# A two-direction RWKV mixer: state walk reordered, one direction's token-laid data in the other half, values reversed by four products

## What is computed

```python
def rwkv7_scan(r, w, k, v, kk, bb, s0, reverse):
    def step(s, inp):
        r_t, w_t, k_t, v_t, kk_t, b_t = inp
        sa = jnp.einsum('bhij,bhj->bhi', s, kk_t)
        s = s * w_t[:, :, None, :] - sa[..., None] * b_t[:, :, None, :] + v_t[..., None] * k_t[:, :, None, :]
        return s, jnp.einsum('bhij,bhj->bhi', s, r_t)
    ...

for d in range(2):
    tc = rwkv_dir_terms(pc[0], pc[1], pc[2], pc[3][d], pc[4][d], ...)
    tl = rwkv_dir_terms(pl[0], pl[1], pl[2], pl[3][d], pl[4][d], ...)
    s_ctx, yc = rwkv7_scan(*tc[:6], zeros, d == 1)
    _, yl = rwkv7_scan(*tl[:6], s_ctx, d == 1)
    oc = oc + yc + tc[6]
    ol = ol + yl + tl[6]
```

## Time and profile before

| | |
|---|---|
| time, median of 3 runs | 2403.95 us (2402.38 to 2406.59) |
| span of the profiled execution | 2404.0 us |
| TensorE busy, weight loads | 2280.8 us, 1700.4 us |
| VectorE, ScalarE, GpSimd busy | 1744.5, 636.9, 236.2 us |
| mean granted TensorE clock | 0.988 of 2.4 GHz |
| first record of the first walk, of the last walk | 1408.3 us, 1889.8 us (L3048) |

### The profile page before, as it was taken

One profiled execution on the slowest core, in us unless ns is written; L12 is line 12 of the kernel. 1 busy time (PEld: TensorE's weight loads), 2 busy tenths in 40 slices (PEclk: granted clock), 3 DMA queues, 4 the chain that ended last, 5 costly groups with the idle time before them and its releaser, 6 DMA issues.

```text
span 2404.0 us, 40144 instructions
## 1 busy us (share of the span) xinstructions
PE 2280.8 (95%) x17202; PEld 1700.4 (71%) x17202; DVE 1744.5 (73%) x2951; ACT 636.9 (26%) x1318; POOL 236.2 (10%) x261
## 2 busy tenths in 40 slices
PE   7999989999997999999999999899998998999998
PEld 3586558888884688888755665766756754768975
DVE  3786477887799888878946869797797425767553
ACT  1314341111002311111033344544444412111111
POOL 2000000201541002024500000000000000000000
PEclk9999999999998999999999999999999999999999
DMA  8232335544532233343313000010010031221102
GB/s 341 74 119 97 140 114 174 172 165 163 177 130 80 79 130 122 135 149 127 118 64 120 23 36 21 23 36 22 21 34 6 20 121 70 88 70 53 36 18 105
DMA packets 43905, 227.95 MB, mean 95 GB/s; under 512 B 4752, under 2 KB 6928, under 8 KB 27600
## 3 DMA queue, kind: packets, MB, share of 16 engines
q1 hardware_dynamic: 23136, 140.56, 16.2%
q0 software_dynamic: 20016, 82.72, 10.1%
q10 hardware_dynamic: 576, 2.11, 0.3%
HBM read 219.07 MB, written 6.29 MB: 94 GB/s over the span
## 4 chain that ended last, share of the span: by engine, by line
PE 83%; DVE 12%; ACT 2%; issue 2%; DMA 1%; POOL 0%; ACTq 0%; DVEq 0%; POOLq 0%
PE ps L692 21%; PE ps L2349 10%; PE ps L914 7%; PE ps L3412 6%; PE ps L2127 3%; PE ps L1048 3%; PE ps L464 2%; PE ps L1747 2%; PE ps L2359 2%; PE ps L2368 2%; PE ps L3666 2%; PE ps L3863 2%; PE ps L3520 2%; PE ps L1249 1%; PE ps L3073 1%
## 5 line engine op out<-in xcount | busy, mean ns | idle before, releaser
L2349 PE MATMUL ps<-H,ring 128*128 128x256 f32 (+1 forms) x832 | 271.4, 487 | 5.4 <-ACT LW L2568 2.6
L692 PE MATMUL ps<-right_sums,left_sums 128*128 128x256 f32 x1056 | 242.8, 379 | 2.7 <-DVE left_sums L672 2.7
L2349 PEld LDWEIGHTS ps<-H,ring 128*128 128x128 f32 x832 | 157.4, 190 | 112.9 <-issue 92.8
L692 PEld LDWEIGHTS ps<-right_sums,left_sums 128*128 128x128 f32 x1056 | 200.5, 190 | 30.6 <-DVE left_sums L672 3.5
L692 PE MATMUL ps<-H,ring 128*128 128x256 f32 x704 | 164.7, 385 | 11.3 <-ACT H L635 11.3
L914 PE MATMUL ps<-G,ring 128*128 128x256 f32 x704 | 159.8, 379 | 0.0
L692 PEld LDWEIGHTS ps<-H,ring 128*128 128x128 f32 x704 | 135.1, 193 | 34.0 <-issue 11.5
L914 PEld LDWEIGHTS ps<-G,ring 128*128 128x128 f32 x704 | 133.8, 190 | 18.2
L384 POOL DMA_DIRECT2D ada_late<-ada_rest x104 | 55.9, 538 | 687.4 <-DVE mod L364 375.0
L759 ACT ACTIVATE C<-U,params_sb 128x512 f32<-128x512 f32 x44 | 35.8, 814 | 315.1 <-DVE U L784 315.1
L692 PE MATMUL ps<-H,left_sums 128*128 128x256 f32 x352 | 87.3, 389 | 0.0
(11 more groups left out here) (655 smaller groups left out, 4969.3 us busy)
## 6 DMA issues: line engine op xcount, KB each, us to landing
ada_late<-ada_rest POOLq DMA_DIRECT2D x104, 512.0 KB, 3.8
ring<-w_up SPq DMA_DIRECT2D x44, 1024.0 KB, 4.8
ring<-w_down SPq DMA_DIRECT2D x16, 1024.0 KB, 4.9
ring<-ev_in SPq DMA_DIRECT2D x15, 1024.0 KB, 4.8
ring<-od_in SPq DMA_DIRECT2D x15, 1024.0 KB, 4.9
ada_early<-ada_rest POOLq DMA_DIRECT2D x24, 512.0 KB, 4.9
ada_first_sb<-ada_first SPq DMA_DIRECT2D x7, 1024.0 KB, 16.4
ring<-ab_in SPq DMA_DIRECT2D x7, 1024.0 KB, 6.2
```

The lines of the kernel that those rows point to most:

```text
L692: return pe.matmul(product(k, n, j), lhsT[:, i, :], rhs[:, i, :], start=(i == 0), stop=(i == 3))
L2349: mm = pe.matmul(k.ps[:, bank + b, 0:tn], wv[:, kk, (i % 2) * P:(i % 2 + 1) * P], k.H[:, kk, t0:t0 + tn], start=(kk == 0), stop=(kk == DT ...
```

## The change

In direction 1 what lies by token goes to the other half: keys' kind in `key_half(h, d)` = half(h ^ d), values' kind in `value_half(h, d)`. So direction 1's right-hand side, solved part and their products move to other tiles of the array. `TOK` is laid by head instead of by kind, and its PSUM banks are 4 + h. The values are no longer flipped one chunk at a time: `values_flipped_pe` makes four products, 512 and 256 columns wide, one pair for each head, and ScalarE puts the chunks in reverse order in two copies; ScalarE's order becomes flipped values, first gather, second token group, two gathers, third token group. In the scores stage the tokens of the first eight units follow the turned values instead of running beside turned and flipped ones. In the walk, right-hand side and solved part share a bank and the state has the other. The kept state is one product for both heads, of the full 128x128 identity with both halves of `SC`, the first of its sum instead of one in the middle, and stands behind the right-hand sides ahead of the solved products, with the values' output products around it; direction 1's state output product joins its values' one. The state's values product waits for the kept one, and each state product (L3091 before) waits for the values' product and for the copy of the solved part. Both right-hand sides' values products follow their state products. In the early output product and at the other places that named it, the token event is numbered anew.

```diff
@@ -2313,6 +2313,14 @@
+def key_half(h, d):
+    return half(h ^ d)
+
+
+def value_half(h, d):
+    return half(1 - (h ^ d))
+
...
 def rw(k, p, j):
@@ -2751,24 +2759,25 @@
         at = slice(c * CK, (c + 1) * CK)
-        for bank, keys, side in ((2 * (n % 2), k.A, 0), (2 * (n % 2) + 1, k.F, 1)):
-            for h in range(2):
-                rhs = k.AR[q % 2][half(h), d, c, :, :].rearrange("p a t -> p (a t)")
-                mm = pe.matmul(k.ps[half(h ^ side), bank, j * 128:(j + 1) * 128], keys[half(h), d, at], rhs, start=True, stop=True)
+        for h in range(2):
+            rhs = k.AR[q % 2][half(h), d, c, :, :].rearrange("p a t -> p (a t)")
+            for bank, keys, home in ((2 * (n % 2), k.A, key_half(h, d)), (2 * (n % 2) + 1, k.F, value_half(h, d))):
+                mm = pe.matmul(k.ps[home, bank, j * 128:(j + 1) * 128], keys[half(h), d, at], rhs, start=True, stop=True)
     mm.then_inc(*k.says(PE, "scores", q, d, i))
-def token_pe(k, u, a):
+def token_pe(k, q, u):
...
     d, c = divmod(u, NK)
-    at = slice(c * CK, (c + 1) * CK)
+    at, to = slice(c * CK, (c + 1) * CK), slice((u % 8) * CK, (u % 8 + 1) * CK)
     for h in range(2):
-        if a:
-            mm = pe.matmul(k.ps[half(h), 5, (u % 8) * CK:(u % 8 + 1) * CK], k.A[half(h), d, at], ident[half(h), :], start=True, stop=True)
-        else:
-            mm = pe.matmul(k.ps[half(1 - h), 4, (u % 8) * CK:(u % 8 + 1) * CK], k.F[half(h), d, at], ident[half(h), :], start=True, stop=True)
-    return mm
+        pe.matmul(k.ps[key_half(h, d), 4 + h, to], k.A[half(h), d, at], ident[half(h), :], start=True, stop=True)
+        mm = pe.matmul(k.ps[value_half(h, d), 4 + h, to], k.F[half(h), d, at], ident[half(h), :], start=True, stop=True)
+        if u % 8 == 7:
+            mm.then_inc(*k.says(PE, "by token mm", q, u // 8, h))
+    if u % 8 == 7:
+        k.mark(PE, "by token mm", q, u // 8)
 def value_turned_pe(k, c):
@@ -2779,13 +2788,13 @@
-def value_flipped_pe(k, c):
-
-    other = 3 - c if c < 4 else 15 - c
-    for h in range(2):
-        mm = k.nc.tensor.matmul(k.ps[half(h), 6 + c // 8, (c % 8) * CK:(c % 8 + 1) * CK], k.r("flip64")[half(h), :], k.VT[half(h), 0, other, :],
-                                start=True, stop=True)
-    return mm
+def values_flipped_pe(k, q):
+
+    for n, (c0, cn) in enumerate(((0, 8), (8, 4))):
+        for h in range(2):
+            mm = k.nc.tensor.matmul(k.ps[half(h), 6 + n, 0:cn * CK], k.r("flip64")[half(1 - h), :], k.VT[half(1 - h), 0, c0:c0 + cn, :].rearrange("p c i -> p (c i)"),
+                                    start=True, stop=True)
+    mm.then_inc(*k.says(PE, "values flipped", q))
 def scores_pe(k, q):
@@ -2799,31 +2808,20 @@
     for c in range(NK):
-        turned = value_turned_pe(k, c)
-        if c < 8:
-            mm = token_pe(k, c, 1)
-        if c == 7:
-            mm.then_inc(*k.says(PE, "by token mm", q, 0))
-    turned.then_inc(*k.says(PE, "values turned", q))
+        mm = value_turned_pe(k, c)
+    mm.then_inc(*k.says(PE, "values turned", q))
+    for u in range(8):
+        token_pe(k, q, u)
     scores_group_pe(k, q, 0, 2)
     pe.wait_ge(*k.when("values", q))
-    for c in range(NK):
-        flipped = value_flipped_pe(k, c)
-        if c < 8:
-            mm = token_pe(k, c, 0)
-        if c == 7:
-            mm.then_inc(*k.says(PE, "by token mm", q, 1))
-    flipped.then_inc(*k.says(PE, "values flipped", q))
+    values_flipped_pe(k, q)
     pe.wait_ge(*k.when("operands", q, 1))
...
     for g in range(1, 3):
-        pe.wait_ge(*k.when("by token", q, 2 * g - 1))
+        pe.wait_ge(*k.when("by token", q, g - 1))
         for u in range(8 * g, 8 * g + 8):
-            kept = token_pe(k, u, 1)
-            mm = token_pe(k, u, 0)
-        kept.then_inc(*k.says(PE, "by token mm", q, 2 * g))
-        mm.then_inc(*k.says(PE, "by token mm", q, 2 * g + 1))
+            token_pe(k, q, u)
         if g == 1:
@@ -2856,9 +2854,11 @@
 def token_act(k, q, g):
-    a, u = k.nc.scalar, 8 * (g // 2)
-    a.wait_ge(*k.when("by token mm", q, g))
-    a.copy(k.TOK[:, u:u + 8, 1 - g % 2, :], k.ps[:, 5 - g % 2, :].rearrange("p (u i) -> p u i", u=8)).then_inc(*k.says(ACTE, "by token", q, g))
+    a, u = k.nc.scalar, 8 * g
+    for h in range(2):
+        a.wait_ge(*k.when("by token mm", q, g, h))
+        a.copy(k.TOK[:, u:u + 8, h, :], k.ps[:, 4 + h, :].rearrange("p (u i) -> p u i", u=8)).then_inc(*k.says(ACTE, "by token", q, g, h))
+    k.mark(ACTE, "by token", q, g)
 def scores_act(k, q):
@@ -2867,16 +2867,15 @@
     token_act(k, q, 0)
+    a.wait_ge(*k.when("values flipped", q))
+    back = by_chunk(flat_ps(k, 6, TA))
+    a.copy(k.VT[:, 1, 0:4, :], back[:, 3::-1, :]).then_inc(*k.says(ACTE))
+    a.copy(k.VT[:, 1, 4:NK, :], back[:, NK - 1:3:-1, :]).then_inc(*k.says(ACTE, "values back", q))
+    gather_act(k, q, 0)
     token_act(k, q, 1)
-    a.wait_ge(*k.when("values flipped", q))
-    a.copy(k.VT[:, 1, :, :].rearrange("p c i -> p (c i)"), flat_ps(k, 6, TA)).then_inc(*k.says(ACTE, "values back", q))
-    gather_act(k, q, 0)
-    token_act(k, q, 2)
-    token_act(k, q, 3)
     gather_act(k, q, 1)
     gather_act(k, q, 2)
-    token_act(k, q, 4)
-    token_act(k, q, 5)
+    token_act(k, q, 2)
 def gather_act(k, p, n):
@@ -2984,8 +2983,7 @@
 def chain_bank(d, c, what):
-    x = c % 2
-    return 2 * d + {"rhs": x, "solved": 1 - x, "state": x}[what]
+    return 2 * d + {"rhs": 0, "solved": 0, "state": 1}[what]
 def chunk_ps(k, h, d, c):
@@ -2997,27 +2995,37 @@
     for h in range(2):
-        mm = k.nc.tensor.matmul(chunk_ps(k, h, d, c), k.VT[half(1 - h), d, c, :], k.SC[half(1 - h), NK * d + c, 3, :], start=True, stop=False)
+        w = value_half(h, d)
+        mm = k.nc.tensor.matmul(chunk_ps(k, h, d, c), k.VT[w, d, c, :], k.SC[w, NK * d + c, 3, :], start=True, stop=False)
+    if d == 1 and c:
+        mm = out_state_pe(k, p, d, c)
     mm.then_inc(*k.says(PE, "out values", p, d, c))
...
+
+def out_state_pe(k, p, d, c):
+
+    for h in range(2):
+        mm = k.nc.tensor.matmul(chunk_ps(k, h, d, c), k.SC[half(h), NK * d + c - 1, 2, :], k.AR[p % 2][half(h), d, c, 1, :], start=False, stop=False)
+    return mm
 def out_pe(k, p, d, c):
...
     pe.wait_ge(*k.when("out values", p, d, c))
-    if c:
-        for h in range(2):
-            pe.matmul(chunk_ps(k, h, d, c), k.SC[half(h), u - 1, 2, :], k.AR[p % 2][half(h), d, c, 1, :], start=False, stop=False)
+    if d == 0 and c:
+        out_state_pe(k, p, d, c)
     for h in range(2):
-        mm = pe.matmul(chunk_ps(k, h, d, c), k.SC[half(h), u, 0, :], k.SC[half(h), u, 1, :], start=False, stop=True)
+        y = key_half(h, d)
+        mm = pe.matmul(chunk_ps(k, h, d, c), k.SC[y, u, 0, :], k.SC[y, u, 1, :], start=False, stop=True)
     mm.then_inc(*k.says(PE, "chunk out", p, d, c))
 def rhs_values_pe(k, p, d, c):
     for h in range(2):
-        mm = k.nc.tensor.matmul(k.ps[half(h), chain_bank(d, c, "rhs"), 0:CK], k.SC[half(1 - h), NK * d + c, 2, :], k.VT[half(1 - h), d, c, :],
-                                start=True, stop=(c == 0))
+        w = value_half(h, d)
+        mm = k.nc.tensor.matmul(k.ps[key_half(h, d), chain_bank(d, c, "rhs"), 0:CK], k.SC[w, NK * d + c, 2, :], k.VT[w, d, c, :], start=True, stop=(c == 0))
     mm.then_inc(*k.says(PE, "rhs values", p, d, c))
@@ -3025,18 +3033,19 @@
 def state_values_pe(k, p, d, c):
+    if c:
+        k.nc.tensor.wait_ge(*k.when("state kept", p, d, c))
     for h in range(2):
-        mm = k.nc.tensor.matmul(k.ps[half(h), chain_bank(d, c, "state"), CK:2 * CK], k.TOK[half(1 - h), NK * d + c, 0, :], k.VT[half(1 - h), d, c, :],
-                                start=True, stop=False)
+        w = value_half(h, d)
+        mm = k.nc.tensor.matmul(k.ps[half(h), chain_bank(d, c, "state"), CK:2 * CK], k.TOK[w, NK * d + c, h, :], k.VT[w, d, c, :],
+                                start=(c == 0), stop=False)
     mm.then_inc(*k.says(PE, "state values", p, d, c))
 def state_kept_pe(k, p, d, c):
-    k.nc.tensor.wait_ge(*k.when("state values", p, d, c))
-    for h in range(2):
-        k.nc.tensor.matmul(k.ps[half(h), chain_bank(d, c, "state"), CK:2 * CK], k.r("ident64")[half(h), :], k.SC[half(h), NK * d + c - 1, 2, :],
-                           start=False, stop=False)
+    k.nc.tensor.matmul(k.ps[:, chain_bank(d, c, "state"), CK:2 * CK], k.c("ident"), k.SC[:, NK * d + c - 1, 2, :], start=True, stop=False)\
+        .then_inc(*k.says(PE, "state kept", p, d, c))
@@ -3048,7 +3057,7 @@
     pe.wait_ge(*k.when("values back", p))
-    pe.wait_ge(*k.when("by token", p, 5))
+    pe.wait_ge(*k.when("by token", p, 2))
     for d in range(2):
@@ -3058,15 +3067,17 @@
                 for h in range(2):
-                    mm = pe.matmul(k.ps[half(h), chain_bank(d, c, "rhs"), 0:CK], k.AR[p % 2][half(h), d, c, 0, :], k.SC[half(h), NK * d + c - 1, 2, :],
+                    mm = pe.matmul(k.ps[key_half(h, d), chain_bank(d, c, "rhs"), 0:CK], k.AR[p % 2][half(h), d, c, 0, :], k.SC[half(h), NK * d + c - 1, 2, :],
```

(35 more changed lines are left out.)

8 lines of the change are left out of this document (4 added, 4 removed).

## The result

| | before | after |
|---|---|---|
| time, median of 4 runs each | 2405.27 us (2402.38 to 2409.95) | 2440.94 us (2437.96 to 2443.81) |
| ratio, 95% interval | | 1.0152 [1.0136, 1.0167] |
| span of the profiled execution | 2404.0 us | 2436.7 us |
| six walks, sum | 166.9 us | 205.7 us |
| five stages between walks, sum | 342.1 us | 336.9 us |

The walks take 38.7 us more, the stages 5.2 less, what is left 0.9 less: 32.7, the difference of the two spans. The last part of the experiments is about why runs of one kernel differ by this much.

A forecast was written before the change was run, and what follows sets the result against it. The walk was taken as a loop, mostly latency, with one place where the queue decides. 2404.0 + 41 (walk steps) - 2 (late instructions) - 3 (stages) = 2440 us, own range 2430 to 2448 at 68%, wider range 2421 to 2452.

The forecast's parts named there:

- Legs of 1.36, 0.68 and 0.83: Walk step, L3061 to L3073 to L3091 to next L3061, each ended by a ScalarE copy; step 2.87 us, was 2.17.
- the rival at 2455: Switches to and from the full product: each waits a whole record, 0.22 not 0.09; 15 us more; chance 6%.
- Hidden weights: Full product's passes in the walk: 128-wide weight loads overlap, a pass is 0.06 us; 13 us less, 2427; chance 15%.
- 41 - 2: Six walks: 41 us more from longer steps, 2 us less from waits for late instructions.
- The first term: Six walks: longer steps, 6.9 us a walk, +41 us in all.
- The second: Walk steps: longer steps leave more time for the next instructions, -2 us, bounds 0 and -2.5.
- Step (4): Stage between walks: four wide flipping products for 24; gather 0.5 us sooner, -3 us in six, bounds 0 and -8.
- The hidden product: Walk: full product fits into ScalarE's round trip, step 2.20 us, stage between walks decides; 2397 to 2402; chance 9%.
- Its second half: Stages between walks then decide: 2402 us, or 2397 to 2398 with an issue wait saved in each, -4 to -5.

The follow-up runs named there:

- e5b: The changed kernel with the full kept product moving 32 of its 64 columns and the kept part left out of the state; 2437.6 us (1 run).
- e9: The kernel before with wide flipping products, keys' tokens placed as before, values' tokens behind, and a later 1 MB weight transfer; 2394.56 us, ratio 0.9958.
- e7: The kernel before with the full-array kept product in its old place and the change's new stage between walks; 2436.52 us (1 run).
- e3: The kernel before with the full-array kept product in its old place, nothing else changed; 2419.21 us, ratio 1.0065.
- e4: The kernel before with the change's new stage between walks alone, walk and halves unchanged; 2404.45 us, ratio 1.0004.
- e8: The kernel before with wide flipping products and reversed copies, keys' tokens placed as before, values' tokens behind the flipping products; 2401.26 us, ratio 0.9994.
- e1: The changed kernel with two 64x64 kept products a direction in place of the full one, same place; 2413.59 us, ratio 1.0039.

## Why the prediction was right, point by point

**The walk, right by its own steps.** Legs of 1.36, 0.68 and 0.83 were forecast and 1.361, 0.688 and 0.828 found. Inside the full product two terms were off and cancel, which is luck. Entering took 0.148, as said. The first pass took 0.16 and not 0.21, so a first full load is hidden in part; the passes behind it are 0.11 apart. From the last one's start to the next small product it took 0.205 and not 0.15. From the first full pass on that is 0.59 against 0.58. The longer way back leans to the rule in the Trainium skill (TensorEngine Tiling (Array Packing), Key Properties), that a change of tiling mode drains TensorE: a pass of this size streams for 0.05 by the estimate in the prediction, and 0.15 beyond it is more than the 0.10 of the earlier trace rows. With half the columns (e5b) the way back is the same 0.206, so it doesn't follow the columns. It is still less than a record's 0.28, so a whole drain at each change, the rival at 2455, isn't seen. Hidden weights, the rival at 2427, would have given 2.66, and e5b shows why not.

**All six walks.** A step rises by 0.35 in the second interval of a walk and by 0.71 in nine; with the walk's end it is 34.28 against the 27.23 of a walk of before without waits for instructions (three of e9's): 42.3 us in six. Before lost 3.6 us to such waits, which are gone: +38.7, forecast 41 - 2. The first term held. The second was 1.6 too small and lies beyond its bound of 2.5, which counted the steps alone; what was lost at the walks' ends came on top.

**The stage, right in sign and wrong in mechanism.** Step (4) gave -0.5 us a stage to the new order and kept one instruction wait in it. The gather was to start 6.3 us after the turned values of the stage before the third walk; it starts after 5.52. The new order by itself costs 0.5 to 0.6 (e7 against e3), so the step that failed is the order's gain. What the stages gained, 5.2 us in five, came from waits for instructions that left them: on the chain to the first gather issue is 0.99 to 1.56 us a stage in before and 0.11 to 0.22 in after. Two things take most of them away, and each does it alone. One is the new stage, with fewer records ahead of the gather: e4, with the walk of before, has 0.71 of the 0.85 us by which after's gather is sooner, and e8 has its gather at 7.02 (whether the number of records or the wide products do it, no run separates). The other is a slower walk ahead: in e3 they left with the old stage and all its records (8.58 to 7.06). The prediction had the first only as a lower bound, one wait of 0.7 us less in each stage for 80 records; it had the second nowhere, and took a wait for instructions to belong to the place where it is seen. The slower walk's share in after is what e4 lacks: no pauses ahead of walks, and 336.9 us of stages against 340.7; that the walk's pace is the reason for this part was not tested.

**The sum.** 2440 against a median of 2440.94. The forecast adds its terms to the profiled span of before, and the span after is 2436.7: 3.3 us less, since the stages gained 2 us more than forecast and small terms 1. The median lies 3.0 us above the profiled run, and a run's time 1.3 above its span. These 4.3 us nearly cancel the 3.3; a hit within 1 us is luck in that part.

**The hidden product**, the rival at 2397 to 2402, asked for under 0.3 us of switches and passes in place of 0.73, and 0.74 were found (0.148 and 0.589); e1, which has only small passes there, shows the step of 2.19 that it named (2.20). Its second half, that then the stage decides with -4 to -5, fails: e1 is at 2413.6, since its walks hold late instructions (29.2 us where the clock left them alone, 27.2 without any) and one the lower clock.

## What to carry to other kernels

A full-array product among 64x64 ones cost the change of mode twice and 0.11 us a pass for its weights, with 64 columns and with 32; with 64 columns two small products were cheaper in both places that were tried. In a loop of tiny products count instructions against time, standalone waits included. A reordering shows its own price only in a version where instructions are not late: try it behind a slower stretch too, as e7 against e3, before believing in its gain. Look at what large transfers run while instructions are fetched. When runs of one kernel scatter, look for a pause of TensorE and the clock behind it before crediting a fraction of a per cent.
